# First block of a three-block transformer kernel: quarters of projections between attention steps, modulation as columns, gating affine moved

## The reference, cut to what matters

```python
sh1, sc1, g1, sh2, sc2, g2 = split(silu(c) @ w_ada + b_ada, 6)       # same for the context
hc = rms_norm(ctx, norm1_g) * (1 + csc1) + csh1                      # 256 rows
k, v, a = hc @ w_in[...]; s_f, s_b = gla_ctx_state(k, v, gates(a))   # start states
h = rms_norm(x, norm1_g) * (1 + sc1) + sh1
q, k, v, a_dn, r, conv_in, sgu_in, gate = split(h @ w_in)
# linear attention, both directions, 4 heads, 8 chunks of 64, state 128 x 256:
#   o_c = q_e @ s + mask(q_e @ k_e.T) @ v;  s = decay * s + k_dec.T @ v
y_a = (rms(o) * gla_norm_g * silu(r)) @ w_o_gla
y_b = silu(layer_norm(depthwise_conv(c1 * sigmoid(c2), 31 taps))) @ w_o_conv
su, sv = split(gelu(sgu_in)); sv = layer_norm(sv) * ln_g + ln_b
y_c = (su * (sgu_ws @ sv + sgu_b)) @ w_o_sgu                         # 8 groups
x = x + g1 * ((sig0 * y_a + sig1 * y_b + sig2 * y_c) @ w_out)
x = x + g2 * swiglu(rms_norm(x) * (1 + sc2) + sh2)
```

## Time and profile before

| | |
|---|---|
| median of three runs | 3838.28 us (3833.26 to 3838.53) |
| the profiled execution | 3838.39 us, its span 3836.5 us |
| TensorE busy | 3650.6 us, 95% of the span |
| VectorE, ScalarE, GpSimd busy | 35%, 33%, 40% |
| mean TensorE clock, granted | 0.956 |

### The profile page before, as it was taken

How to read it: one execution, slowest core, us unless ns; L and a number is a source line. 1 busy time by engine, 2 the same in 40 slices (tenths; PEclk the granted TensorE clock), 3 DMA queues, 4 the chain that set the end, 5 groups by cost and what they waited for, 6 DMA issues and landing times.

```text
span 3836.5 us, 39091 instructions
## 1 busy us (share of the span) xinstructions
PE 3650.6 (95%) x16080; PEld 2890.0 (75%) x16080; DVE 1343.5 (35%) x2083; ACT 1249.3 (33%) x1924; POOL 1552.1 (40%) x725
## 2 busy tenths in 40 slices
PE   6999978988989999999999999999999999999999
PEld 3677766767768888888767788888877777887766
DVE  2223699674321112211155311111112542112564
ACT  2520222224232223222344422232223443222453
POOL 2330334454644444445531444544454224444322
PEclk8896889999989999999999999999999999999899
DMA  5210112434432332233311223323332113233211
GB/s 202 77 61 1 55 61 76 155 132 154 159 102 97 98 95 94 99 95 98 95 40 34 96 97 93 100 95 99 94 102 85 33 41 102 95 93 104 66 42 53
DMA packets 98718, 342.21 MB, mean 89 GB/s; under 512 B 11180, under 2 KB 11436, under 8 KB 98125
## 3 DMA queue, kind: packets, MB, share of 16 engines
q1 hardware_dynamic: 97776, 335.06, 26.8%
q10 hardware_dynamic: 764, 4.66, 0.3%
HBM read 337.06 MB, written 2.10 MB: 88 GB/s over the span
## 4 chain that ended last, share of the span: by engine, by line
PE 82%; DVE 11%; ACT 3%; POOL 2%; issue 1%; DMA 0%; ACTq 0%; DVEq 0%
PE ps L1029 21%; PE ps L1031 21%; PE ps L1030 21%; DVE t L1959 6%; PE ps L1264 3%; PE ps L1288 2%; PE ps L1191 1%; POOL t L2314 1%; PE ps L1048 1%; PE ps L1049 1%; PE ps L1050 1%; PE ps L1203 1%; PE ps L1275 1%; PE ps L1066 1%; DVE t L1853 1%
## 5 line engine op out<-in xcount | busy, mean ns | idle before, releaser
L2314 POOL TENSOR_TENSOR t<-t,t 128x1024 fp32r<-128x1024 f32 (+2 forms) x588 | 1358.5, 2312 | 1918.6 <-ACT t L1349 1918.3
L1029 PE MATMUL ps<-t,t 128*128 128x512 f32 (+1 forms) x4048 | 1617.0, 399 | 88.1 <-POOL t L2314 61.5
L1030 PE MATMUL ps<-t,t 128*128 128x512 f32 (+1 forms) x4048 | 1595.5, 394 | 0.0
L1031 PE MATMUL ps<-t,t 128*128 128x512 f32 (+1 forms) x4048 | 1594.5, 394 | 0.0
L1029 PEld LDWEIGHTS ps<-t,t 128*128 128x128 f32 x4048 | 773.7, 191 | 274.6 <-issue 57.8
L1031 PEld LDWEIGHTS ps<-t,t 128*128 128x128 f32 x4048 | 772.2, 191 | 165.0
L1030 PEld LDWEIGHTS ps<-t,t 128*128 128x128 f32 x4048 | 773.2, 191 | 155.6 <-issue 0.7
L1349 ACT CAST t<-t 128x1024 fp32r<-128x1024 f32 (+2 forms) x588 | 583.0, 995 | 464.2 <-PE ps L1031 339.9
L2118 DVE TENSOR_TENSOR t<-t,ps 128x512 f32<-128x512 f32 x110 | 75.6, 687 | 568.7 <-PE ps L1031 560.5
L1410 ACT CAST t<-t 128x512 fp32r<-128x512 f32 x158 | 96.2, 620 | 489.1 <-DVE t L2118 404.5
L1959 DVE SCALAR_TENSOR_TENSOR t<-t,t,t 128x392 f32<-128x392 f32 (+14 forms) x240 | 239.9, 1000 | 7.8
(11 more groups left out here) (264 smaller groups left out, 2627.2 us busy)
## 6 DMA issues: line engine op xcount, KB each, us to landing
t<-in_w_f1i SPq DMA_DIRECT2D x88, 512.0 KB, 3.3
t<-in_w_f2i SPq DMA_DIRECT2D x88, 512.0 KB, 3.3
t<-in_w_ada SPq DMA_DIRECT2D x72, 512.0 KB, 4.2
t<-in_w_ffi SPq DMA_DIRECT2D x44, 512.0 KB, 3.2
t<-in_w_f1o SPq DMA_DIRECT2D x32, 512.0 KB, 3.5
t<-in_w_f2o SPq DMA_DIRECT2D x32, 512.0 KB, 3.5
t<-in_w_gate SPq DMA_DIRECT2D x24, 512.0 KB, 3.5
t<-in_w_out SPq DMA_DIRECT2D x48, 256.0 KB, 2.6
```

Of the source, the lines that this page charges most:

```text
L1029: e.matmul(out, wh[:, at], X.hi[c][:, 0:N], start=c == first, stop=False)
L1030: e.matmul(out, wh[:, at], X.lo[c][:, 0:N], start=False, stop=False)
L1031: m = e.matmul(out, wl[:, at], X.hi[c][:, 0:N], start=False, stop=c == final)
L2314: e.tensor_tensor(k.WL[:, n % NHL, 0:w], k.raw[:, j % NRAW, 0:w], f(k.WH[:, n % NHL, 0:w]), ALU.subtract).then_inc(*k.rest.inc(('rest', j) ...
```

## The change

Only `first` and what it calls change; the half-unit helper of the later blocks is generalised to parts and does the same there.

- Modulation: `ada_rows` holds the weights and moves the two columns of `c`, 8 matmuls per piece, straight into columns. Norm roots and rows stand between the pieces of the second group. `norm_tile` is split in `norm_scale` and `norm_parts`.
- The gates of x, the first queries and keys and one conv pair move into the context stage. Logarithms and values come for two heads at a time.
- One buffer set serves all heads. `chain` is cut into steps, and 72 quarters of units (conv 1 to 7, queries and keys 2 and 3), 18 per head, stand between the pieces. Taps start beside the first values.
- The sums of `ada_sum` start with the r units. The gating unit's values, its norm and `su` move into and behind branch 0. Gain and shift of its norm are applied behind the spatial product, with a bias made of `sgu_b`, the shift and the sums of `sgu_ws`. Two 512 KB loads disappear.

```diff
     def ada_rows(self, g, kt):
-        for half in range(2):
-            b = self.take(k.banks, 'ada', g, half) if kt == 0 else self.bank('ada', g, half)
-            m = e.matmul(b[0:2, :], cc[:, :, kt], k.raw[:, i % NRAW, half * 512:half * 512 + 512], start=kt == 0, stop=kt == KT - 1)
+        b = self.take(k.banks, 'adac', g, hold=True) if kt == 0 else self.bank('adac', g)
         for n in range(8):
-            m = e.matmul(b[:, 2 * n:2 * n + 2], k.ROW[0:2, g, n * 128:n * 128 + 128], const(k, 'ident', 2)[:, 0:2], start=True, stop=True)
+            m = e.matmul(b[:, 2 * n:2 * n + 2], k.raw[:, i % NRAW, n * 128:n * 128 + 128], cc[:, :, kt], start=kt == 0 and n == 0, stop=kt == KT - 1, skip_group_check=True)
...
+    def beside(n):
+        for i in range(n):
+            next(quarters, None)
+            on.taps(1 + i % 2)
     for h in range(4):
...
+        if h == 2:
+            on.head_logs(1)
+            for kp in range(4):
+                on.K(('v', 1), 'v', 1, XA, kp, 4)
+                on.taps(5)
+            for tt in range(4):
+                on.value(1, tt)
+        on.prepare(h)
+        if h:
+            on.head_scale(0, h - 1)
+        beside(2)
+        on.decayed(h)
+        beside(2)
+        on.inner(h)
+        if h:
+            on.head_scale(1, h - 1)
+        beside(4)
+        on.masked(h)
+        beside(2)
+        on.chain_begin(h)
+        for step in range(8):
+            on.chain(h, step)
+            if h and step == 3:
+                on.head_scale(2, h - 1)
+            beside(1)
+        on.chain_end(h)
...
+    for i in range(KT):
+        on.T(('r', i), 'r', i, XA)
+        on.taps(5)
+        ada()
+        if i < 3:
+            on.head_scale(i, 3)
+        on.gla_out(i)
...
+    for i in range(KT + LEAD):
+        if i < KT:
+            on.T(('gate', 0, i), 'gate', i, XA)
+            on.taps(5)
             ada()
+            on.gate(0, i)
+        sgu_norm(3 if i > 6 else 0)
+        if i >= LEAD:
+            on.T(('ogla', i - LEAD), 'ogla', i - LEAD, k.OG)
+            on.taps(5)
+            ada()
+            on.gated(0, 'ogla', i - LEAD)
+        sgu_norm(3 if i > 6 else 0)
+        if i in (5, 6):
+            on.taps(999)
+            for kp in range(4):
+                on.K(('sv', i - 5), 'sv', i - 5, XA, kp, 4)
+                ada()
+            for tt in range(4):
+                on.sgu_in(i - 5, tt)
...
     def sgu_in(self, n, tt):
         self.wait_ge('filled', (('sv', n), tt))
+        self.wait_ge('tap', 7, 30)
...
         if step[0] == 'a':
-            e.scalar_tensor_tensor(row, row, st[:, 24 + tt:25 + tt], k.SG2, ALU.mult, ALU.mult).then_inc(*k.dve.inc())
-            e.tensor_tensor(row, row, k.SGB, ALU.add).then_inc(*k.dve.inc(('sgu normed', tt)))
+            e.tensor_scalar(row, row, st[:, 4 + tt:5 + tt], st[:, 24 + tt:25 + tt], ALU.add, ALU.mult).then_inc(*k.dve.inc(('sgu normed', tt)))
```

More of the change, by code:

```diff
@@ L352, in norm @@
     elif j < 10:
[L353 to L361, removed]
+        on.norm_scale(m, j - 2)
+        on.norm_parts(m, j - 2)
 def first(on, k):
@@ L439, in first, with projections @@
-    on.sgu_loads()
+    on.head_logs(0)
+    for kp in range(4):
+        on.K(('v', 0), 'v', 0, XA, kp, 4)
+        on.taps(6)
+    for tt in range(4):
+        on.value(0, tt)
+    for w, name in enumerate('qk'):
+        on.T((name, 1), name, 1, XA)
+        on.taps(6)
+        on.query_key(1, w)
+    def projections():
+        for n, i in (('conv', 1), ('qk', 2), ('conv', 2), ('qk', 3), ('conv', 3), ('conv', 4), ('conv', 5), ('conv', 6), ('conv', 7)):
+            for w in range(2):
+                key, name, tile = ((('c2', i), 'conv', 8 + i), (('c1', i), 'conv', i))[w] if n == 'conv' else (('qk'[w], i), 'qk'[w], i)
+                for part in range(4):
+                    on.T_part(key, name, tile, XA, part, 4)
+                    if part == 3 and n == 'qk':
+                        on.query_key(i, w)
+                    if part == 3 and n == 'conv':
+                        (on.conv_in if w else on.conv_gate)(i)
+                    yield
@@ L440, in first @@
+    for _ in quarters:
+        on.taps(2)
     side = iter([('ada', g, kt) for g in (2, 3, 4, 5) for kt in range(KT)] + [('ada3', g, kt) for g in range(3) for kt in range(KT)])
@@ L526, in branch @@
             on.gate(g, i)
-        if i == LEAD - 1 and middle is not None:
-            middle()
         if i >= LEAD:
@@ L1173, in chain @@
             for v in range(2):
[L1174 to L1175 removed]
+                e.matmul(bo[v][:, at], k.VT[:, t, w + v * 128:w + v * 128 + 128], k.AM[:, at], start=t == 0, stop=False, skip_group_check=True)
+    def chain(self, h, step):
+        k, e = (self.k, self.e)
         for d in range(2):
[L1177 removed]
@@ new lines, in chain @@
+            c = step if d == 0 else 7 - step
+            at = slice(64 * c, 64 * c + 64)
+            if step == 0:
+                state = k.SIN[:, d, h, :]
+                self.wait_ge('copied state', d, h)
+            else:
+                state = gla_ring(k).of(('st', h, d))[:, 256 * ((step - 1) % 2):256 * ((step - 1) % 2) + 256]
+                self.wait_ge('state', h, d, step - 1)
+            for v in range(2):
+                m = e.matmul(self.bank('bo', h, v)[:, at], state[:, v * 128:v * 128 + 128], k.QE[:, d, at], start=False, stop=step == 7 and d == 1, skip_group_check=True)
@@ L1222, in ada_sum, with sgu_norm @@
         m.then_inc(*k.filled.inc(('filled', (name, g))))
+    def sgu_norm(self, step):
+        k, e = (self.k, self.e)
+        if step == 'bias':
+            for i in range(2):
+                b = self.take(k.banks, 'ws', i)
+                self.wait_ge('load', 'sgu ws')
+                e.matmul(b, const(k, 'one'), k.WS[:, 4 * i:4 * i + 4, :].rearrange('p g n -> p (g n)'), start=True, stop=True).then_inc(*k.filled.inc(('filled', ('ws', i))))
     def spatial(self, g):
@@ L2000, in sgu_norm @@
             return
+        if step == 'bias':
+            o = COL['sgu_b'][0]
+            self.wait_ge('load', 'sgu bias')
+            for g in range(8):
+                at = slice(128 * (g % 4), 128 * (g % 4) + 128)
+                self.wait_ge('filled', ('ws', g // 4))
+                e.scalar_tensor_tensor(k.BG[g // 4][:, at], self.bank('ws', g // 4)[:, at], k.col[:, o + g:o + g + 1], k.BG[g // 4][:, at], ALU.mult, ALU.add).then_inc(*k.dve.inc(('sgu bias', g), *([('free', ('ws', g // 4))] if g % 4 == 3 else [])))
+            return
         if step == 'r':
```

533 lines of the change are left out of this document (272 added, 261 removed).

## The result

The changed kernel takes **3845.84 us** (median of 9 runs, 3840.27 to 3855.6), the kernel before 3836.05 us (9 runs, 3833.26 to 3838.53): a ratio of 1.0031, 95% interval 1.002 to 1.0043. It is slower by 0.3%, where 3788 was forecast with a range that ended at 3828. The profiled execution took 3845.66 us (span 3843.5), 7.3 more than that of before.

The account below looks back on a forecast made before the run. The prediction saw VectorE's convolution taps setting the pace in part of the first block, a lowered TensorE clock in the linear attention, and TensorE full from 1200 us. +16 - 10 - 56 + 17 - 17 = -50 gave 3788 us, range 3748 to 3828.

Parts of the forecast that it names:

- A: Modulation: slower by 16 us, small column matmuls at half clock, first projection at 82 us instead of 65.84.
- B: Context stage: 10 us gained, from 76 to 66 us, with bounds of 0 to 20 gained.
- C: From x's gates to the first r projection: 56 us gained, from 387 to 331 us.
- whether the clock holds: Linear attention heads: full clock assumed with quarters between the chain's steps; the point on which C rests.
- the 3 x 4.5 named: Heads in C: stalls of 4.5 us for each of three heads, as one head's buffers no longer alternate.
- Rival 3: Heads: VectorE's order stalls TensorE, 13 us per head and a clock falling after each wait; 3823 us, 14%.
- rival 2: Heads: the mixed chain does not hold the clock, TensorE keeps 0.69, 108 us more; 3896 us, 5%.
- D: The r units and first branch: 17 us lost, 183 us for 22 units instead of 166, VectorE's taps setting the pace.
- E: Rest of the first block: 17 us gained, from the gating norm's wait (7.5) and sum-step waits (9); bounds 0 to 30.
- rival 1: Modulation: full clock there, so A is -15 instead of +16; 3757 us, 12%.
- rival 4: Tap stage is not VectorE's: with taps at their median D gains 15 instead of losing 17; 3756 us, 9%.
- Rival 5: Whole kernel: the gains move only, VectorE's total unchanged; within 7.7 us of 3838, 3%.

Follow-up runs that it names:

- experiment 2: The changed kernel with the modulation made as rows of 512 columns again, in the change's order: 3832.87 us, 0.999 of the kernel before.
- experiment 1: The changed kernel with no tap ahead of a head's seven mask operations, its six taps moved into the chain's first six steps: 3804.49 us, 0.9913.
- experiment 3: The changed kernel with the modulation sums' 24 steps moved from the r projections and first branch to after the second gating values: 3818.6 us, 0.9936.
- experiment 9: The kernel before with 64 unused bytes per partition set aside behind the table of columns: 3842.85 us, 1.0019.
- experiment 4: The changed kernel with the edits of experiment 1, experiment 2 and experiment 3 together, and eight taps fewer beside each set of values: 3762.55 us, 0.9802.
- experiment 5: As experiment 1, but three of the six taps stay ahead of the mask operations: 3813.23 us, 0.9943.
- experiment 6: As experiment 1, but the eight quarters of a head stand behind its chain instead of between its steps: 3846.05 us, 1.0021.
- experiment 10: The changed kernel with 64 more unused bytes behind the table of columns: 3853.68 us, 1.0058.
- experiment 13: The changed kernel with its large arrays at the place they have in the kernel before: 3832.89 us, 0.9995.

## Why the prediction was wrong, point by point

**A was right in mechanism and nearly in size.** It came to +12.3 for +16, and experiment 2 confirms where it comes from: 16.1 us for the columns, less 3.8 for the new order of the norms. The small matmuls ran 207 ns apart (3.31 us for sixteen, 3.57 forecast from the row at 44.47 us). The forecast that the clock would *read* near 0.5 was wrong: it reads 1.00.

**B and C failed, at one step: "whether the clock holds".** The loss to the half clock stood at nothing, and it was 48.9 us. I decided the step by the row of 1900 to 2000 us, where projections stand among small matmuls without any wait, and added the waits only at their own length. The other terms were near: 350.8 us of work for 355, 44.2 idle for 42. Of the waits that is in part luck: the masks' 14.7 us are near the 3 x 4.5 named, but the 11.4 at the value copies I had not named. One term was also misread, without harm to the sum: the 0.137 us of the earlier trace rows is the shortest duration of a weight load, not the pitch of a matmul.

What experiment 1 takes away fits: with the taps behind the masks (experiment 1) the first silu of r comes at 488 us; the forecast of 479 for the unit means 484. Rival 3 had the mechanism ("13 us per head, and a clock that falls after each wait") and rival 2 nearly the size (it decides below a clock of 0.83; 200 to 522 us average 0.86), but I priced them as separate cases, 14% and 5%. How much of the 47 us falls to B alone stays open.

The Trainium skill (TensorE: Matmul & The Clock Gate, HAM oscillation - how this bites in real kernels) describes the first part of this: a wait throws the clock back, and the next piece of work starts slow. The trace agrees, with the clock at 0.50 behind the waits of 2.19 and 4.40 us; it adds that the half clock then lasted 30.7 us, although TensorE was busy all along from 309.06 us on.

**D was right.** It came to +18 for +17: the r units are 8.05 us apart ((583.81 - 527.44) / 7) against 8.1 forecast, VectorE is busy 66.28 of 69 us, and the gap at the burst is 13.27 us against 17. What stood for the loss was right too: experiment 3 took the sums out and gained 27 us.

**E was half right.** It came to -8 for -17. The wait of 10.57 us at 837.87 gave way to waits for GpSimd of 3.9 us and less, but the sums' small matmuls still wait in the later branches (8.5 us in 3 waits behind 704 us): moving sum steps earlier made fewer of them late, not none.

**Outside the prediction: the place.** That everything after the first block is untouched was true of the instructions, not of the addresses. It cost 4.6 us in the profile, and experiment 9 shows 7.1 us for the same 64 bytes in the kernel before.

Of the rivals, 1 and 4 (full clock in the modulation, tap stage not VectorE's) are refuted by the 333 ns loads and by a VectorE that is 96% busy in the r units. Rival 5, that gains only move, names the measured time (7.4 us from 3838.4), but by luck: experiments 1 to 4 add up, so gains do not only move.

## What to carry to other kernels

A wait of TensorE of some 4 us can cost several times its length, because of the clock behind it. So sum the waits and then ask of each what runs behind it: in the traces of the change and of experiments 1, 2, 5, 6, 10 and 13, waits of 4.8 to 7.1 us ahead of a head's preparation were never followed by more than 6.8 us of half clock, while 4.05 us ahead of a chain were followed by 34.1. Filler on another engine belongs behind the operations that TensorE waits for, never ahead of them, even where that engine's total is far from the bound; here that order alone decided between 3846 and 3804 us (experiment 1). A change that lengthens a table moves everything placed behind it, so compare matmul counts in a saturated stretch of untouched code before looking for a cause in the change.

## What the runs showed of the hardware that I had not expected

**The column of the granted clock can read 1.00 where TensorE runs at half rate.** Ahead of 71 us of the changed kernel every weight load of 128 x 128 takes 333 ns, against 189 in the last chain, and the page reads 1.00 there (columns: busy us, mean ns):

```profile
L1119 PEld LDWEIGHTS ps<-t,t 128*128 128x128 f32 x249 | 53.7, 333 | 0.0
...
L1081 PEld LDWEIGHTS ps<-t,t 128*128 128x128 f32 x18 | 3.4, 189 | 0.4
```

The trace holds no record of the clock there. The first begins at 82.5 us, just where the projections' matmuls go from 0.43 to 0.23 us apart, and the view fills the time ahead of it with 1.00. The kernel before has its first record at 17.0 us, where its wide matmuls speed up (7 in the five us ahead of it, 13 in the five behind). The load's duration is the better gauge, and with it the 1.2 GHz level can be told without the column. The Trainium skill (TensorE: Matmul & The Clock Gate, Seeing it yourself) warns that the clock records of a trace can be unreliable. Here they agree with the durations wherever there are any; it is their absence that misleads.

**The place of a moving operand changes a matmul's pitch** at full clock: 227 ns at before's place, 229 with 64 bytes more, 233 with 128 bytes more or less. All of these places are multiples of 64 bytes, and those 128 bytes off are, like before's, multiples of 128, so neither rule separates good from bad.

**The clock can fall with TensorE 100% busy**: in the first head's bare chain (experiment 6) it went to 0.50 at 258.1 us, 10 us after the last wait and with none between. With a quarter of a projection between the steps (experiment 1) it did not.
